# Item 8 of the conditioning weights: multiplied and added by GpSimd, summed by one set of products

## The reference, cut to what matters

```python
c_act = jax.nn.silu(c)                          # (1, 1024)
for i in range(2):
    mod = c_act @ ada_w[i] + ada_b[i]           # ada_w[i]: (1024, 6144)
    sh_m, sc_m, g_m, sh_f, sc_f, g_f = split(mod, 6)
    h = rmsnorm(x) * (1.0 + sc_m) + sh_m
    x = x + g_m * mixer_i(h)                    # layer 0: pooling, layer 1: attention
    h = rmsnorm(x) * (1.0 + sc_f) + sh_f
    x = x + g_f * hier_moe(h)                   # 32 experts, two of them per token
out = rmsnorm(x)
```

## Time and profile before

| | |
|---|---|
| median of 3 runs | 760.78 us (760.22 to 762.2) |
| profiled execution | 762.43 us, span 760.7 us |
| TensorE busy | 712.6 us, 94% of the span |
| VectorE, ScalarE, GpSimd busy | 232.6, 164.8, 39.7 us |
| read from HBM | 273.17 MB, 360 GB/s over the span |
| granted TensorE clock | 0.996 of full speed |

### The profile page before, as it was taken

The page is one execution under the profiler, slowest core; times in us unless marked ns, Lnnn a source line. Parts: engine busy times, 40 slices in busy tenths (PEclk is TensorE's granted clock), DMA queues, the critical chain, the costliest instruction groups (busy, mean ns, idle before and its releaser), DMA issues.

```text
span 760.7 us, 12156 instructions
## 1 busy us (share of the span) xinstructions
PE 712.6 (94%) x4474; PEld 408.1 (54%) x4474; DVE 232.6 (31%) x640; ACT 164.8 (22%) x378; POOL 39.7 (5%) x71
## 2 busy tenths in 40 slices
PE   4798899999889999989999999999999998999995
PEld 1444455554454545437877877655555554455542
DVE  1025533222211212143674862373322221121213
ACT  4014431111101111142323322253111110111113
POOL 0000011110000000000000000000000000000000
PEclk9999999999999999999999999999999999999999
DMA  8999999999999999999588539583999999999951
GB/s 356 409 416 411 414 419 411 417 416 419 415 419 414 417 417 417 415 395 373 243 291 341 199 111 394 198 348 131 411 394 417 416 418 416 417 416 416 414 238 57
DMA packets 61234, 274.90 MB, mean 361 GB/s; under 512 B 4481, under 2 KB 17921, under 8 KB 39553
## 3 DMA queue, kind: packets, MB, share of 16 engines
q1 hardware_dynamic: 61184, 274.23, 89.8%
HBM read 273.17 MB, written 1.05 MB: 360 GB/s over the span
## 4 chain that ended last, share of the span: by engine, by line
PE 80%; DMA 14%; SPq 2%; DVE 2%; ACT 1%; issue 1%; DVEq 0%; ACTq 0%
PE bank L533 71%; DMA ring<-in_exp_w_up_dram 8%; PE bank L688 4%; DMA ring<-in_ada_w_dram 3%; DMA reg_a<-in_band_dram 3%; PE bank L675 2%; SPq L392 1%; PE bank L802 1%; PE bank L1009 1%; DVE ye L1502 0%; SPq L389 0%; ACT reg_h L1148 0%; DVE reg_a L1505 0%; PE bank L663 0%; PE bank L927 0%
## 5 line engine op out<-in xcount | busy, mean ns | idle before, releaser
L533 PE MATMUL bank<-ring,xe 128*64 128x256 f32 x1984 | 229.5, 384 | 10.8 <-DMA ring<-in_exp_w_up_dram 9.2
L533 PEld LDWEIGHTS bank<-ring,xe 128*64 128x64 f32 x1984 | 141.6, 137 | 82.4 <-issue 15.5
L533 PE MATMUL bank<-ring,heT 128*64 128x512 f32 x512 | 123.9, 604 | 0.0
L1502 DVE TENSOR_TENSOR reg_c<-reg_c,bank 128x128 f32<-128x128 f32 x64 | 18.5, 288 | 271.9 <-ACT reg_c L1216 271.9
L505 POOL COPY xe<-reg_a 128x512 f32 x62 | 38.2, 617 | 666.5 <-PE bank L533 370.9
L1148 ACT ACTIVATE ye<-bank 128x512 f32<-128x512 f32 (+1 forms) x72 | 41.7, 585 | 139.4 <-PE bank L533 139.2
L1216 ACT ACTIVATE reg_c<-bank 128x128 f32<-128x128 f32 x64 | 17.8, 278 | 249.1 <-PE bank L533 246.3
L533 PE MATMUL bank<-reg_b,ring 128*128 128x256 f32 x256 | 58.2, 381 | 0.8 <-ACT reg_b L1360 0.8
L1502 DVE TENSOR_TENSOR reg_b<-bank,colp 128x512 f32 x64 | 44.3, 692 | 44.2 <-issue 36.8
L533 PEld LDWEIGHTS bank<-ring,heT 128*64 128x64 f32 x512 | 31.2, 136 | 47.2 <-issue 47.0
L533 PE MATMUL bank<-ring,cact 128*32 128x512 f32 (+1 forms) x320 | 36.1, 548 | 19.1 <-DMA ring<-in_ada_w_dram 17.2
(11 more groups left out here) (164 smaller groups left out, 513.7 us busy)
## 6 DMA issues: line engine op xcount, KB each, us to landing
ring<-in_exp_w_gate_dram SPq DMA_DIRECT2D x64, 1024.0 KB, 15.3
ring<-in_exp_w_up_dram SPq DMA_DIRECT2D x64, 1024.0 KB, 17.4
ring<-in_exp_w_down_dram SPq DMA_DIRECT2D x64, 1024.0 KB, 14.0
ring<-in_ada_w_dram SPq DMA_DIRECT2D x48, 1024.0 KB, 13.1
ring<-in_w_qkv_dram SPq DMA_DIRECT2D x12, 1024.0 KB, 13.1
ring<-in_w_o_dram SPq DMA_DIRECT2D x4, 768.0 KB, 5.6
x_sb<-in_x_dram SPq DMA_DIRECT2D x1, 1024.0 KB, 5.2
reg_a<-in_band_dram SPq DMA_DIRECT2D x1, 1024.0 KB, 19.8
```

Source lines behind the costliest of these rows:

```text
L533: return nc.tensor.matmul(o_, l_, r_, start=start, stop=stop)
L1502: return nc.vector.tensor_tensor(o_, a_, b_, op)
```

## The change

GpSimd gets item 8. Behind its memset in layer 0 it multiplies the three thirds by their columns of `cact`, the first into `acc[0]`, the other two into `acc[1]`, each then added to `acc[0]`, and then frees slot 1. TensorE drops the three thirds of item 8; third (9,0) now opens the sum in bank 2. One `sums_of` behind third (10,1) adds the accumulator to the same bank and signals `part_full`. The order of the remaining thirds on TensorE is moved up.

```diff
+            def item_8():
+                s, turn = ADA_AT[8]
+                dst = acc[:, 0, :]
+                for r in range(3):
+                    third_full(pool, 8, r)
+                    product = dst if r == 0 else acc[:, 1, :]
+                    if r:
+                        pool.wait_ge(S("acc_pool"), 2 * r - 1)
+                    nc.gpsimd.tensor_scalar(product, third_w(s, r), cact[:, r:r + 1], None, ALU.mult).then_inc(S("acc_pool"), 1)
+                    if r:
+                        pool.wait_ge(S("acc_pool"), 2 * r)
+                        nc.gpsimd.tensor_tensor(dst, dst, product, ALU.add).then_inc(S("acc_pool"), 1)
+                pool.wait_ge(S("acc_pool"), 5)
+                pool.sem_inc(S("ring_free", s), 1)
+                pool.sem_inc(S("down_free", s), 1)
...
                 if L == 0:
                     nc.gpsimd.memset(rwA, 0.0).then_inc(S("rwA_clear"), 1)
+                    item_8()
...
-                                  w[:, u, q, :], k == 0, k == KC - 1)
+                                  w[:, u, q, :], k == 0 or (a, i) == (9, 0), k == KC - 1 and n != 4)
...
-                    last.then_inc(S("part_full"), 1)
+                    if n != 4:
+                        last.then_inc(S("part_full"), 1)
...
-            def sums_of(dst, g):
-                pe.wait_ge(S("acc_step"), 2 * KC * (g + 1))
+            def sums_of(dst, g, more=False):
+                if more:
+                    pe.wait_ge(S("acc_pool"), 5)
+                else:
+                    pe.wait_ge(S("acc_step"), 2 * KC * (g + 1))
                 for q in range(4):
-                    last = mm(dst[32 * q:32 * q + 32, 0:512], ones[:, 0:32], acc[:, g, q * 512:(q + 1) * 512], True, True)
+                    last = mm(dst[32 * q:32 * q + 32, 0:512], ones[:, 0:32], acc[:, g, q * 512:(q + 1) * 512], not more, True)
...
                 down_of(L, E - 1, *loaded(L, E - 1), 1)
+                turn_ye_of(L, E - 1, 1)
                 if L == 0:
                     pe.wait_ge(S("dn_free", L), E + 1)
-                    third(8, 0, 4)
-                turn_ye_of(L, E - 1, 1)
-                if L == 0:
-                    third(8, 1, 4)
+                    third(9, 0, 4)
...
-            third(8, 2, 4)
-            third(9, 0, 4)
             third(9, 1, 4)
+            third(9, 2, 4)
+            third(10, 0, 4)
             pe.wait_ge(S("x_rows"), 4)
             pe.wait_ge(S("xr_act"), 2)
             pe.wait_ge(S("xr_dve"), 2)
             turn_rows(0)
             turn_rows(1)
-            third(9, 2, 4)
-            third(10, 0, 4)
             third(10, 1, 4)
+            sums_of(bank[2], 0, True).then_inc(S("part_full"), 1)
             turn_rows(2)
             turn_rows(3)
             columns(4)
```

## The result

The changed kernel takes 768.12 us (median of 4 runs, 766.93 to 769.1) against 761.49 us before on the same chip: 1.0083 times the time, 95% interval 1.0062 to 1.0104. It is 6.6 us slower; the forecast was 759.8, the range 758.3 to 762.8. The profiled execution has a span of 767.0 us, 6.3 more than before.

What follows compares the result with a forecast made beforehand. TensorE was taken to bound the kernel, with 80% of the chain. Gains of 0.14 and 0.82 us sum to 0.96 us off its path, from the median 760.78 to 759.8 us; range 758.3 to 762.8.

Steps and rivals of the forecast that it cites:

- part 4: GpSimd's three products and two additions on item 8: 15.2 us from 324.0, done at 339.2, ends 333.4 and 344.3.
- margin of 4.9 us: Before TensorE's sums, wanted at about 344.1: GpSimd done at 339.2, so the new wait costs nothing.
- the late GpSimd: At TensorE's sums: GpSimd's operations need 25 us, end at 349, and the kernel takes 764.8 us; chance 9%.
- my sum: GpSimd's five operations: 3 x 2.17 + 2 x 4.24 + five hand-overs of 0.05 = 15.2 us.
- costs each us beyond: At TensorE's sums: a GpSimd end past 345.0 costs each microsecond beyond it.
- The held addition: VectorE's two-SBUF-input sum of squares at 337.07 waits for GpSimd's last addition: net 0.2 us slower, 761.0; chance 22%.
- GpSimd's upper end: GpSimd ends at 344.3; second tile's addition waits, VectorE's last half starts near 345.0, 3.6 us stall, net 2.7 slower.
- My sign for a hold: VectorE's sum of squares starting right when a GpSimd operation ends, with idle time ahead of TensorE's first turns.
- Parts 1 and 3: TensorE's tail of the last experts gains 0.14 us; between the turns, 1.89 us replaces 2.71, gaining 0.82.
- part 2: TensorE after the combine: three thirds before and now, no difference; the 1.90 us pause stays, all thirds land in time.
- the pause's vanishing: TensorE after the combine: with 16 fewer records ahead, the 1.90 us pause may vanish, giving 757.9; chance 9%.
- Part 5: Queues: GpSimd frees slot 1 at 339.2; the second qkv item, issued only at 342.62, is not delayed.

Runs made afterwards that it cites:

- 2, one-input sums of squares: Changed kernel with VectorE's sum of squares as a reduction with one SBUF input instead of two: 768.91 us, 1.0082 times before.
- 5, kept busy: Changed kernel with three unused 512-column products on TensorE before the waits for the turned rows and three before the sums: 765.68 us, 1.0053 times before.
- 6, GpSimd started earlier: Changed kernel with GpSimd's five operations moved ahead of the wait for the last expert: 768.52 us in one run.
- 7, other operations on GpSimd: Changed kernel with GpSimd's three multiplications replaced by a copy, a two-input multiplication and a multiplication by 0.5 (result wrong): 767.4 us in one run.
- 1, short GpSimd work: Changed kernel with GpSimd's five operations replaced by one memset of the accumulator (item 8's share left out): 759.13 us, 0.9963 times before.
- 8, ScalarE's products: Changed kernel with the three products made by ScalarE in place, GpSimd doing only the two additions: 758.94 us, 0.9968 times before.
- 10, GpSimd alone, quicker: Changed kernel with GpSimd started earlier, multiplying by two-input operations, and VectorE's sums of squares as one-input reductions: 758.69 us, 0.9963 times before.
- experiments 3: Kernel before, TensorE's eight thirds kept, with GpSimd's five operations on item 8 added and their result unused: 764.86 us, 1.0033 times before.
- experiment 4: Kernel before with GpSimd's five operations added unused, and VectorE's sums of squares as one-input reductions: 763.95 us, 1.0023 times before.
- experiment 9: Kernel with ScalarE's products plus four unused 4-column products (eight records) in TensorE's wait for the last ye: 761.55 us, 0.9982 times before.

## Why the prediction was wrong

| kernel | sums start | to the turn of x | from there to landmark | landmark | against before |
|---|---|---|---|---|---|
| before | - | - | - | 523.38 | |
| changed | 350.04 | 11.81 | 170.18 | 532.03 | 1.0083 |
| 2, one-input sums of squares | 349.99 | 11.32 | 171.86 | 533.17 | 1.0082 |
| 5, kept busy | 349.95 | 8.20 | 170.19 | 528.34 | 1.0053 |
| 6, GpSimd started earlier | 347.46 | 9.61 | 171.87 | 528.94 | one run |
| 7, other operations on GpSimd | 349.42 | 9.00 | 171.87 | 530.29 | one run |
| 1, short GpSimd work | 343.37 | 8.19 | 170.18 | 521.74 | 0.9963 |
| 8, ScalarE's products | 343.20 | 8.19 | 170.18 | 521.57 | 0.9968 |
| 10, GpSimd alone, quicker | 343.50 | 8.19 | 170.17 | 521.86 | 0.9963 |

The turn of x is the group at 361.85 in the changed kernel. The fourth column is the same in all but experiments 2, 6 and 7, where the 16 records near 490 took 1.69 us more at a lower granted clock. All twelve profiled executions have the same pause of 1.20 us in front of these records, and only these three have the low clock behind it; why is not shown.

The 8.65 us at the landmark add up from the runs: TensorE's new order -1.64; sums at 350.04 and not 343.37, +6.67; low clock +3.62 (11.81 - 8.19 us). That is 8.65.

**The step that failed is part 4, the size of GpSimd's product.** I took 2.17 us from the copy, with 2.47 as the upper end; it measured 5.44. A whole copy of 2,048 columns does take 1.89 us, so the scaling of the copy was near and the inference from copy to multiplication was not. My bound was no bound: I let two inputs cost up to three passes, but held one input at four copies, and no row excluded a slow operation. Three products at 5.44 and not 2.17 us are 9.8 of the 10.7 us by which the sum fell short. The margin of 4.9 us in front of the sums, which rested on it, was gone. The addition was near: 4.52 us against my 4.24. The Trainium skill (GPSIMD Engine Reference, Performance versus the Vector engine) has 4,497 ns for it; the trace has 4.50 to 4.55 us, within about 1%.

**The rival that came true is the late GpSimd**, to which I gave 9%. It was worked for an end of 349 (1.65 times my sum); the end was 349.99 (1.70 times). Its price, 4.0 us, lacked one term: what idle TensorE does to the granted clock. With 1.0 us more for the later end and 3.6 for the clock, 4.0 becomes 8.6, against 8.65 at the landmark. My "costs each us beyond" was the wrong price for this wait.

**The held addition is also real, but was not what cost.** Experiments 2 to 4 separate it: two additions held behind GpSimd in the changed kernel, all but 0.5 us masked by the later wait at the sums. The Trainium skill (SBUF - State Buffer, Who interferes with whom) says that a VectorE instruction with two SBUF inputs contends with a GpSimd instruction that reads SBUF, and that of two contending instructions the one that came first keeps the shared port for its whole length while the other is fully blocked. For GpSimd's additions the trace agrees: VectorE ends at 339.80 with GpSimd at 339.78, and in experiment 4 at 349.95 with 349.92. For its multiplications it does not: VectorE was let through 3.7 us after their start, with 1.7 us left to run. I gave it 22%, and as an alternative to lateness; both stem from long GpSimd operations and came together. Experiment 7 happens to be my case of GpSimd's upper end (forecast 344.3, here 344.36): VectorE's last half starts at 344.94, as I had it (near 345.0), but TensorE stands 4.45 us and not 3.6, since the shorter pause brings it there earlier, and the low clock comes on top, which I had priced at nothing here too. My sign for a hold was a late start; what it shows as is a long duration.

**Parts 1 and 3 held, and part 2 but for the pause.** The turn of the last ye at 329.96, the combine at 331.61 (forecast 329.88 and 331.53); all thirds had landed; third plus sums take 1.86 us in experiment 1 (342.49 to 344.35; forecast 1.89). The landmark gain of 1.64 us against 0.96 is the shorter pause, which part 2 had left at 1.90. I had the pause's vanishing as a rival at 9%, for the reason that fewer records stand ahead; that reason is shown by experiment 9, but only 0.8 us of the pause went, and the records fewer are eight (third (8,0)), not the 16 that I wrote. **Part 5 held only in effect:** slot 1 came free at 350.2 and not 339.2, SP waited 7.7 us for GpSimd, and TensorE still waited for no transfer in attention.

**What came back behind the landmark.** 8.65 us there are 6.3 at the end. Before has this in layer 1's experts:

```profile
641.28 5.36 PE L533 MATMUL bank<-ring,xe 128*64 128x256 f32 x32 [2.17 <-DMA ring<-in_exp_w_up_dram]
```

Behind the wait of 2.17 us the granted clock is 0.58 from 642 to 646, and the 32 records take 5.36 us. In the changed kernel such a group takes 3.67 us, its waits there are at most 1.3 us and the clock stays at 1.00. That is 1.7 of the 2.3 us; the rest is lost ahead of it. From landmark to end take 237.3 us before, 237.5 to 237.9 in experiments 3, 4 and 6, which have the same dip, and 234.8 to 235.7 in all the others, which have not. What decides whether it comes in an execution stays open. So a good part of the 0.3% of experiments 8 and 10 may be this dip and not the change: the profiled executions are 3.8 to 3.9 us apart from before's, and only 1.5 to 1.8 us of that lie ahead of the landmark. These are the change's own.

## What to carry to other kernels

Where an engine gets a kind of instruction that the trace does not show, measure it by itself before placing it: here a multiplication by a scalar on GpSimd took 2.9 times as long as a copy of the same size, and the same product written with two inputs a third less. Work moved off a busy engine must be done before that engine comes for it, with its real duration; count a TensorE wait of several us with its length and with the low clock behind it (3.6 us here), and see whether products that end before the wait does can fill it, as in experiment 5. From 40 us to the end of all twelve profiled executions, each of the ten waits of 2.1 us and more had a low clock behind it where the clock was up before; behind shorter ones it was mixed. And look for small VectorE instructions with both inputs in SBUF under a long GpSimd addition or multiplication: they are held, and whoever waits for them too.

## What the runs showed of the hardware that I had not expected

- On GpSimd, for 128x2048 float32: copy 1.89 us, multiplication by a scalar 5.44 (from SBUF) and 5.37 (fixed), two-input multiplication with a repeated column 3.60, two-input addition 4.52. The memset of this size took 1.81 us in experiment 1.
- A GpSimd multiplication by a scalar held VectorE's instruction with two SBUF inputs for 3.7 us from its start in five cases (339.95 to 343.68, 340.04 to 343.75, 339.86 to 343.58, 337.38 to 341.11, and 334.41 to 338.06 with the fixed number), not for its 5.4 us. A hold does not show as idle time of VectorE but as a long duration of a tiny instruction: 128x1 in 2.65 us. VectorE's reductions with one input ran in 0.14 us beside the same operations, and an operation with one input in PSUM and one in SBUF was not held either (0.69 us at 327.59 in the changed kernel).
- TensorE's pause behind the combine ended 7.8 to 8.0 us behind the combine's start, wherever it began: behind 6 records it lasted 1.9 to 2.0 us, behind 14 records 1.0 to 1.15. What TensorE waits for there is not shown.
- ScalarE can multiply 2,048 columns by a column in 2.00 us, at 321 to 329 in gaps that the experts leave, without any of its copies being late (the ye copy at 329.26, before at 329.23).
